# Attention stage: ScalarE takes the exponentials of a chunk's rows right behind that chunk's hi copy, and no longer behind the hi copy of the next chunk

## The chip, the cores and the metric

One core of a Trainium2 chip. The metric is the device time of one execution of the whole program, in microseconds; three runs of the kernel before gave 2290.93, 2291.99 and 2295.94 us, median 2291.99. The numbers of the profile come from one more execution, taken with the hardware profiler.

## What is computed

One transformer layer in fp32: adaptive norm and projections, a causal "forgetting" attention, a short convolution, an output projection, and a mixture of experts (32 experts, 4 for each token). Only the attention matters here. It has 8 heads of 64 columns over 1024 positions:

```
s = einsum('bhqd,bhkd->bhqk', q_block, k[:q1]) * scale      # a block is 128 queries
s = s + cum[q] - cum[k];  s = where(k_pos <= q_pos, s, -inf)
p = softmax(s);  out = p @ v[:q1]
```

The layer starts with `rms_norm(x) * (1 + sc1) + sh1`, where `sc1`, `sh1` and four more vectors come from `silu(c) @ w_ada`; part of that product is made on GpSimd beside the attention.

## The kernel before, in words

The program runs in four stages, each an `nc.Block()` with one instruction stream per engine and a meeting of all engines at its end: projections, attention (`attention_block`, L682), mixer, experts. Every engine takes its instructions strictly in the order written; semaphores tie the streams together.

**Rows and chunks.** Head h has 8 query blocks i = 0 to 7; row block n = 8h + i needs scores of width 128(i+1). Four blocks form a unit (i = 0 to 3, and i = 4 to 7). The probabilities of a unit are transposed key block by key block; one such step is a chunk. A head has 12 chunks, k = 0 to 11: k = 0 to 3 are the first unit (transposed width 512, 384, 256, 128) and k = 4 to 11 the second (512 five times, then 384, 256, 128). There are 96 chunks; below, c is the number over all heads and k the number within a head.

**What a chunk does**, engine by engine:
- TensorE: `turn(c)` transposes (L943), into one of three PSUM banks used in a ring; at k = 3 and 7 `fold_out` of the unit before (L970); then `scores(n)` for the row blocks in `scored[c]` (L928 to L931), into one of two pairs of banks, which waits for `exp(n-2)`; then `values(c-2)` (L959), the product with v of two chunks ago.
- ScalarE: `pthi`, the hi copy of the transposed chunk (L850), which waits for `turn(c)`; at k = 1 and 5 `copy_out` of the unit before (L841); then exponentials (L833), each with a read of the row sum behind it; and at 8 of the chunks from c = 48 on (every fifth: 48, 53, 58, 63, 68, 73, 78, 83) a copy of a piece of `w_out` for the next stage (L859).
- VectorE: `ptlo`, the lo part (L893), which waits for the hi copy of this chunk; at k = 3 and 7 `finish` of the unit before (L880, L883); then `lowest(n)` for the rows in `scored[c]` (a row reduction of the scores, L873), on which `exp(n)` waits; at k = 3 also a reciprocal for the mixer (L869), which stands behind the rest.

**Which rows in which chunk.** `scored` (L707 to L711) puts one row block into each of eight chunks: i = 6 and 7 of this head at k = 0 and 1, and of the next head i = 0, 1, 2, 3 at k = 4 to 7, i = 4 at k = 9, i = 5 at k = 11. Chunks 2, 3, 8 and 10 have none. The first six row blocks come ahead of chunk 0. `turn` of chunk k = 4 waits until i = 7 has its exponential, and that of k = 0 until i = 3 of its head has it.

**ScalarE's order before.** In chunk c it makes the hi copy of c and only then the exponentials of the rows scored in chunk c-1 (L854):

```
for n in scored[c - 1] if c else ():
    exp(n)
```

GpSimd meanwhile works through 16 pieces of `w_ada` (L818, L820, two buffers); SyncE loads q, k and v of later heads (L784 to L796), each when the scores or values of an earlier head are done.

Of the kernel before, what the change touches and what calls it, by code (L numbers as in the profile page):

```python
# [681 lines left out]
def attention_block(nc, s, a):  # L682
# [10 lines left out]
    NCH = len(chunks)  # L693
# [4 lines left out]
    def first(c):  # L698
        u, kt = chunks[c]
        return max(0, kt - QB * (u % 2))  # L700

    def through(u):
        return sum(QB * (v % 2 + 1) for v in range(u + 1))
# [3 lines left out]
    scored = {c: [] for c in range(NCH)}  # L707
# [11 lines left out]
    def copied(c):  # L719

        u, kt = chunks[c]
        return u - 1 if kt == 1 and u else None
# [16 lines left out]
    with ExitStack() as ctx:  # L739
# [23 lines left out]
        def probs(n):  # L763
            h, i = n // NT, n % NT
            return pr_short[:, i, :] if i < QB else pr_long[h % 2][:, i - QB, :]

        def scores_bank(n):
            L = (n % NT + 1) * P
            return psum[:, 2 * (n % 2):2 * (n % 2) + 2, :].rearrange("p b n -> p (b n)")[:, 0:L]

        with nc.Block() as block:
            @block.sync
            def _(sp):
                def load_values(h):

                    sp.dma_start(vhl[h % 2][:, :, :].bitcast(F32),
                                 s.v_d[:, h, :, :].rearrange("(t p) s n -> p t (s n)", p=P)).then_inc(v_in[h % 2], 16)

                load_values(0)
                for h in range(1, H):  # L780
                    i, rows = h % 2, slice(h * HD, (h + 1) * HD)
                    if h >= 2:
                        sp.wait_ge(s_mm, NT * (h - 1))
                    sp.dma_start(q1[i][0:HD, :].bitcast(F32), s.q_d[0, rows, :]).then_inc(qk_in[i], 16)  # L784
                    sp.dma_start(q1[i][HD:P, :].bitcast(F32), s.q_d[1, rows, :]).then_inc(qk_in[i], 16)
                    for half in (0, HD):
                        sp.dma_start(k1[i][half:half + HD, :].bitcast(F32), s.k_d[0, rows, :]).then_inc(qk_in[i], 16)
                    if h == 1:
                        sp.wait_ge(pad_ok, 2)
                    sp.dma_start(q2[i][0:HD, :].bitcast(F32), s.q_d[0, rows, :]).then_inc(qk_in[i], 16)  # L790
                    sp.dma_start(k2[i][0:HD, :].bitcast(F32), s.k_d[1, rows, :]).then_inc(qk_in[i], 16)
                    for dst, src in ((q2, s.extq_d), (k2, s.extk_d)):
                        sp.dma_start(dst[i][HD:HD + 4, :].bitcast(F32), src[h, :, :]).then_inc(ext_in[i], 16)
                    if h >= 2:
                        sp.wait_ge(pv_mm, through(2 * h - 3))
                    load_values(h)  # L796
                    if h == 2:
                        sp.dma_start(s.slab[:, :, :], a["w_out"][0].rearrange("(k p) n -> p k n", p=P)[:, :, 0:s.HALF]
                                     ).then_inc(slab_in, 16)
                sp.wait_ge(slab_in, 16)  # L800
# [23 lines left out]
            @block.scalar  # L824
            def _(act):
                def exp(n):
                    h, i = n // NT, n % NT
                    act.wait_ge(mn_ok, n + 1)
                    if i < QB and h >= 1:
                        act.wait_ge(pt_mm, through(2 * h - 2))  # L830
                    if i >= QB and h >= 2:
                        act.wait_ge(pt_mm, through(2 * h - 3))
                    nc.scalar.activation(probs(n)[:, 0:(i + 1) * P], scores_bank(n), ACT.Exp, bias=mn[:, n:n + 1],  # L833
                                         scale=-1.0, accum_out=rsum[:, n:n + 1]).then_inc(exp_ok, 1)

                def copy_out(u):

                    act.wait_ge(pv_mm, through(u))
                    if u >= 2:
                        act.wait_ge(fold_mm, u - 1)  # L840
                    nc.scalar.activation(outT[u % 2][:, :], psum[:, OB, :], ACT.Copy).then_inc(outT_ok, 1)  # L841

                for n in early:
                    exp(n)
                for c in range(NCH):
                    w = (QB - first(c)) * P
                    act.wait_ge(pt_mm, c + 1)
                    if c >= R:
                        act.wait_ge(pv_mm, c - R + 1)
                    nc.scalar.activation(pthi[c % R][:, 0:w], psum[:, TB + at_ring["chunk", c] % 3, 0:w],  # L850
                                         ACT.Copy).then_inc(pthi_ok, 1)
                    if copied(c) is not None:
                        copy_out(copied(c))
                    for n in scored[c - 1] if c else ():  # L854
                        exp(n)
                    if c in split_at:
                        k = split_at.index(c)
                        act.wait_ge(slab_in, 16)
                        nc.scalar.activation(s.whi0[:, k, :], s.slab[:, k, :], ACT.Copy)  # L859
                for n in scored[NCH - 1]:  # L860
                    exp(n)
                copy_out(NU - 1)

            @block.vector
# [1477 lines left out]
```

## Time and profile before

| | us |
|---|---|
| median of three runs | 2291.99 |
| profiled execution, its time | 2300.91 |
| profiled execution, its span | 2299.2 |
| TensorE busy | 2178.1 (95%) |
| VectorE busy | 1756.1 (76%) |
| ScalarE busy | 1358.2 (59%) |
| GpSimd busy | 815.7 (35%) |
| attention stage | 380.2 to 547.7 |

Busy time is the sum of the durations of an engine's instructions. TensorE's mean granted clock over the execution was 0.975 of full speed. The attention stage is 167.5 us of the span, 7%; most of the rest is the expert stage.

### The profile page before, as it was taken

Reading aid. Unit: us, or ns where it says so; the run is one execution under the profiler, and the core shown is the slowest. Engines: PE = TensorE matmul, PEld = TensorE weight load, DVE = VectorE, ACT = ScalarE, POOL = GpSimd, SP = SyncE. Lnnn points to the kernel's source line nnn. Section 1 sums busy time; section 2 is a strip of 40 time slices with the busy share of each in tenths; the row PEclk is TensorE's granted clock in tenths of the full one; section 3 lists DMA queues with packets and bytes.
Section 4 is the critical chain, followed back from the end, with each engine's and each line's share of the span. In section 5 each row is a group of like instructions: output and inputs, shape, how many; then the busy total and the mean of one; then the engine's idle time right before and its main releaser. Section 6 shows DMA issues by size and latency. Waiting matters only on the chain.

```text
span 2299.2 us, 37071 instructions
## 1 busy us (share of the span) xinstructions
PE 2178.1 (95%) x10302; PEld 1799.2 (78%) x10303; DVE 1756.1 (76%) x2165; ACT 1358.2 (59%) x1859; POOL 815.7 (35%) x804
## 2 busy tenths in 40 slices
PE   5999997888977899999999999999999999999997
PEld 4678885776865788888888888888888888888885
DVE  5683422676775799977799977788999779798897
ACT  4332211575325577766667766676777666677675
POOL 2263003885134234432224422142444322144241
PEclk9899998899988999999999999999999999999999
DMA  7233205883336899997789988797999878899794
GB/s 268 87 115 138 60 19 121 239 230 109 115 125 235 285 367 365 379 355 271 267 295 374 384 295 269 237 358 270 387 376 371 324 265 310 286 359 386 258 382 159
DMA packets 299090, 603.19 MB, mean 262 GB/s; under 512 B 24720, under 2 KB 46240, under 8 KB 295392
## 3 DMA queue, kind: packets, MB, share of 16 engines
q1 hardware_dynamic: 270912, 528.95, 64.1%
q0 software_dynamic: 27072, 69.40, 10.9%
q10 hardware_dynamic: 1056, 4.19, 0.5%
q8 instruction: 28, 0.46, 0.1%
q14 instruction: 22, 0.18, 0.0%
HBM read 563.71 MB, written 44.53 MB: 265 GB/s over the span
## 4 chain that ended last, share of the span: by engine, by line
PE 65%; DMA 2%; issue 1%; DVE 0%; POOL 0%; POOLq 0%; DVEq 0%; ACT 0%; ACTq 0%
PE psum L2255 60%; PE psum L2194 2%; PE psum L2237 2%; PE psum L2202 2%; DMA d_xg<-xn_d,d_entry 1%; DMA d_entry<-list_d 1%; POOL d_spare L1846 0%; POOL d_roww L1903 0%; DVE d_wlo L2073 0%; DVE d_yst L2126 0%; DVEq L1738 0%; ACT d_whi L1930 0%; POOLq L1689 0%; POOLq L1690 0%; POOLq L1842 0%
## 5 line engine op out<-in xcount | busy, mean ns | idle before, releaser
L2073 DVE TENSOR_TENSOR d_wlo<-d_raw,d_whi 128x1024 fp32r<-128x1024 f32 x578 | 676.7, 1219 | 127.7 <-ACT d_whi L1930 125.4
L1930 ACT ACTIVATE d_whi<-d_raw 128x1024 fp32r<-128x1024 f32 x578 | 579.8, 1054 | 62.7 <-PE psum L2255 49.7
L2255 PE MATMUL psum<-d_whi,d_xthi 128*128 128x512 f32 x1152 | 455.5, 395 | 6.1 <-issue 6.1
L2255 PE MATMUL psum<-d_whi,d_xtlo 128*128 128x512 f32 x1152 | 450.2, 391 | 0.0
L2255 PE MATMUL psum<-d_wlo,d_xthi 128*128 128x512 f32 x1152 | 449.9, 391 | 0.0
L1835 POOL DMA_INDIRECT out_dram<-d_yst,d_dest x49 | 149.7, 3055 | 665.2 <-DVE d_yst L2126 660.5
L2073 DVE TENSOR_TENSOR d_wlo<-slab,d_whi 128x1024 fp32r<-128x1024 f32 x292 | 343.8, 1219 | 21.6 <-ACT d_whi L1930 19.2
L1930 ACT ACTIVATE d_whi<-slab 128x1024 fp32r<-128x1024 f32 x292 | 292.3, 1054 | 7.7 <-PE psum L2255 6.1
L2255 PEld LDWEIGHTS psum<-d_whi,d_xthi 128*128 128x128 f32 x1152 | 217.3, 189 | 51.8 <-issue 8.0
L2255 PEld LDWEIGHTS psum<-d_whi,d_xtlo 128*128 128x128 f32 x1152 | 217.1, 188 | 46.3
L2255 PEld LDWEIGHTS psum<-d_wlo,d_xthi 128*128 128x128 f32 x1152 | 217.4, 189 | 43.6
L2255 PE MATMUL psum<-d_whi,d_athi 128*128 128x512 f32 x576 | 228.7, 397 | 0.0
L2255 PE MATMUL psum<-d_whi,d_atlo 128*128 128x512 f32 x576 | 224.6, 390 | 0.0
L2255 PE MATMUL psum<-d_wlo,d_athi 128*128 128x512 f32 x576 | 224.5, 390 | 0.0
L1972 ACT ACTIVATE d_athi<-psum 128x512 fp32r<-128x512 f32 x72 | 43.1, 599 | 181.6 <-PE psum L2202 170.9
L2255 PE MATMUL psum<-d_whi,d_xt 128*128 128x512 f32 x384 | 150.3, 391 | 0.0
L2255 PE MATMUL psum<-d_wlo,d_xt 128*128 128x512 f32 x384 | 150.1, 391 | 0.0
L2255 PEld LDWEIGHTS psum<-d_whi,d_atlo 128*128 128x128 f32 x576 | 108.2, 188 | 23.1
L1819 POOL DMA_INDIRECT d_xg<-xn_d,d_entry x48 | 68.2, 1422 | 162.0 <-DMA d_entry<-list_d 152.3
L2255 PEld LDWEIGHTS psum<-d_wlo,d_athi 128*128 128x128 f32 x576 | 108.3, 188 | 21.0
L2255 PEld LDWEIGHTS psum<-d_whi,d_athi 128*128 128x128 f32 x576 | 108.3, 188 | 20.0
L1826 POOL DMA_INDIRECT d_rowt<-topw_d,d_entry x72 | 95.6, 1328 | 41.7 <-POOL d_dest L1857 28.2
(351 smaller groups left out, 4010.8 us busy)
## 6 DMA issues: line engine op xcount, KB each, us to landing
slab<-in_w_gate_up_dram SPq DMA_DIRECT2D x144, 1024.0 KB, 8.4
d_raw<-in_w_gate_up_dram SPq DMA_DIRECT2D x144, 1024.0 KB
d_raw<-in_w_down_dram SPq DMA_DIRECT2D x144, 1024.0 KB
b_wp<-in_w_ada_dram POOLq DMA_DIRECT2D x16, 1024.0 KB, 9.4
slab<-in_w_in_dram SPq DMA_DIRECT2D x12, 1024.0 KB, 5.4
d_bias_rows<-in_b_gate_up_dram SPq DMA_DIRECT2D x12, 1024.0 KB
d_bias_rows<-in_b_down_dram SPq DMA_DIRECT2D x12, 512.0 KB
a_xin<-in_x_dram ACTq DMA_DIRECT2D x2, 2048.0 KB
```

What stands on the lines that cost most here:

```text
L1819: pool.indirect_dma_start(out=xg[b][:, :], out_offset=None, in_=src[:, :], in_offset=bass.IndirectOffsetOnAxis(ap=index, axis=0)).then_inc ...
L1826: pool.indirect_dma_start(out=rowt[b][:, :], out_offset=None, in_=s.topw_d[:, :], in_offset=bass.IndirectOffsetOnAxis(ap=entry[b][0:ROWS[b ...
L1835: pool.indirect_dma_start(out=s.out, out_offset=bass.IndirectOffsetOnAxis(ap=dest[b][:, :], axis=0), in_=yst[b][:, :], in_offset=None, com ...
L1930: nc.scalar.activation(whi[n % NW][:, part, :], raw[n % NRAW][:, part, :], ACT.Copy).then_inc(whi_ok, 1)
L1972: nc.scalar.activation(athi[:, 4 * i:4 * i + 4, :].rearrange("p k n -> p (k n)"), psum[:, 6, :], ACT.Copy).then_inc(athi_ok, sh)
L2073: nc.vector.tensor_tensor(wlo[n % NW][:, part, :], raw[n % NRAW][:, part, :], whi[n % NW][:, part, :].bitcast(F32), ALU.subtract).then_inc ...
L2194: mm = nc.tensor.transpose(turned_x[:, k, :], xg[b][:, k * P:(k + 1) * P], s.ident[:, :])
L2202: mm = nc.tensor.transpose(psum[:, 6 + b, t * P:(t + 1) * P], act_t[b][:, t * P:(t + 1) * P], s.ident[:, :])
L2237: mm = nc.tensor.matmul(to[0:ROWS[b], :], pick[:, 0:ROWS[b]], bhl[:, at:at + SL], start=False, stop=last)
L2255: mm = nc.tensor.matmul(to, m_[:, KH * h + k, :], w_[n % NW][:, k, :], start=(h == 0 and k == 0 and q == 0 and not loaded), stop=(h == 1 a ...
```

## The change

In chunk c ScalarE now makes the hi copy of c, then `copy_out` where there is one, and then the exponentials of the rows scored in the same chunk. The loop behind the last chunk goes, because nothing is left for it. The other engines' streams, the buffers and the number of instructions stay as they are.

```diff
                     if copied(c) is not None:
                         copy_out(copied(c))
-                    for n in scored[c - 1] if c else ():
+                    for n in scored[c]:
                         exp(n)
                     if c in split_at:
                         k = split_at.index(c)
                         act.wait_ge(slab_in, 16)
                         nc.scalar.activation(s.whi0[:, k, :], s.slab[:, k, :], ACT.Copy)
-                for n in scored[NCH - 1]:
-                    exp(n)
                 copy_out(NU - 1)
```

## Rows read from the trace of the kernel before

**Rows 1.** Busy time by stretch: stretch, length, each engine's busy us, TensorE clock, DMA.

```profile
380.20:547.70 167.50, 142.74 (x864) 121.18 (x864) 108.93 (x200) 104.95 (x249) 141.99 (x50) 0.92 0.75 206
```

**Rows 2.** Waits in 380 to 550: who waited for whom, us, times, longest.

```profile
PE psum L943 <- ACT b_pr_long L833: 4.7, 8, 1.8
PE psum L928 <- ACT b_pr_short L833: 3.7, 9, 0.6
PE psum L928 <- ACT b_pr_long L833: 3.6, 7, 0.9
```

**Rows 3.** Timeline, end of the stage: start, length, engine, line, operation.

```profile
541.52 4.58 POOL L820 TENSOR_TENSOR modacc<-modacc,b_wp 128x2048 f32<-128x2048 f32 x1
547.21 0.43 DVE L883 TENSOR_TENSOR attn<-psum,b_rsum 128x256 f32<-128x256 f32 x1
```

**Rows 4.** Timeline 501 to 520: instructions of one head on ScalarE and VectorE.

```profile
501.59 0.36 ACT L833 ACTIVATE b_pr_short<-psum,b_mn 128x128 f32<-128x128 f32 x1
501.93 0.60 ACT L850 ACTIVATE b_pthi<-psum 128x512 fp32r<-128x512 f32 x1
...
503.76 0.60 ACT L850 ACTIVATE b_pthi<-psum 128x512 fp32r<-128x512 f32 x1 [0.78 <-PE psum L943]
...
504.39 0.69 DVE L893 TENSOR_TENSOR b_ptlo<-psum,b_pthi 128x512 fp32r<-128x512 f32 x1 [0.67 <-ACT b_pthi L850]
...
505.00 0.17 DVE L880 RECIPROCAL b_rsum<-b_rsum 128x4 f32<-128x4 f32 x1
...
505.54 0.68 DVE L873 TENSOR_REDUCE b_mn<-psum 128x1 f32<-128x512 f32 x1
...
510.73 0.29 DVE L893 TENSOR_TENSOR b_ptlo<-psum,b_pthi 128x128 fp32r<-128x128 f32 x1 [0.79 <-ACT b_pthi L850]
...
510.94 0.95 DVE L873 TENSOR_REDUCE b_mn<-psum 128x1 f32<-128x768 f32 x1
...
511.92 0.90 ACT L833 ACTIVATE b_pr_long<-psum,b_mn 128x768 f32<-128x768 f32 x1 [0.73 <-DVE b_mn L873]
...
515.96 0.63 ACT L859 ACTIVATE whi<-slab 128x512 fp32r<-128x512 f32 x1
516.48 0.38 ACT L850 ACTIVATE b_pthi<-psum 128x256 fp32r<-128x256 f32 x1
...
516.74 1.12 ACT L833 ACTIVATE b_pr_long<-psum,b_mn 128x1024 f32<-128x1024 f32 x1
516.89 0.42 DVE L893 TENSOR_TENSOR b_ptlo<-psum,b_pthi 128x256 fp32r<-128x256 f32 x1 [1.41 <-ACT b_pthi L850]
...
517.83 0.29 ACT L850 ACTIVATE b_pthi<-psum 128x128 fp32r<-128x128 f32 x1
...
518.16 0.29 DVE L893 TENSOR_TENSOR b_ptlo<-psum,b_pthi 128x128 fp32r<-128x128 f32 x1 [0.84 <-ACT b_pthi L850]
...
518.91 0.94 DVE L869 RECIPROCAL crs<-crs 128x128 f32<-128x128 f32 x1
...
519.77 0.63 DVE L893 TENSOR_TENSOR b_ptlo<-psum,b_pthi 128x512 fp32r<-128x512 f32 x1
```

**Rows 5.** Timeline: hi copies of chunks 7, 14 and 86.

```profile
407.64 0.60 ACT L850 ACTIVATE b_pthi<-psum 128x512 fp32r<-128x512 f32 x1 [1.89 <-PE psum L943]
...
419.32 0.38 ACT L850 ACTIVATE b_pthi<-psum 128x256 fp32r<-128x256 f32 x1
...
534.65 0.38 ACT L850 ACTIVATE b_pthi<-psum 128x256 fp32r<-128x256 f32 x1
```

**Rows 6.** A wait of TensorE for a load (timeline).

```profile
441.74 0.48 PE L928 MATMUL psum<-b_k,b_q 128*128 128x128 f32 x1 [2.00 <-DMA b_k<-k_d]
```

**Rows 7.** Busy time by stretch, with TensorE's clock.

```profile
440.00:445.00 5.00, 3.26 (x15) 3.26 (x16) 2.00 (x4) 0.96 (x2) 3.54 (x1) 0.65 1.08 250
445.00:450.00 5.00, 4.84 (x25) 4.06 (x25) 2.57 (x6) 3.08 (x9) 4.62 (x3) 0.67 1.02 274
...
499.28:518.48 19.20, 16.62 (x111) 14.04 (x110) 13.45 (x26) 13.42 (x33) 16.40 (x6) 1.00 0.78 213
```

## The prediction, made before the changed kernel ran

> **What bounds the stage now.** I read the busy times by stretch first, then the waits, then the timeline of one head. The edit touches ScalarE's order between 380 and 547.7 us and nothing else, so only that stage counts. There TensorE is busy 142.7 of 167.5 us, VectorE 108.9, ScalarE 105.0, GpSimd 142.0 [rows 1]: no engine is full, TensorE is nearest. The waits show what it lacks: it waits for an exponential 3.7 + 3.6 + 4.7 = 12.0 us in all [rows 2], because scores(n) needs exp(n-2), and turn of chunk k = 4 needs the exponential of i = 7. A head takes 19.2 us: between the hi copies of chunks 14 and 86, six heads apart, lie 534.65 - 419.32 = 115.3 us [rows 5]. The stage ends with VectorE's last write at 547.64; GpSimd, which does its own work beside it, ends at 541.52 + 4.58 = 546.10 [rows 3], 1.5 us earlier, and the next stage waits for both.
>
> **What the order of before buys.** In chunk c ScalarE copies hi(c), then waits for nothing of this chunk: the exponential it takes is of the chunk before. Meanwhile VectorE makes lo(c) and the reduction of the new rows. The two engines work side by side, one chunk apart.
>
> **What the edit makes of it.** exp(n) now stands ahead of hi(c+1), and it needs the reduction of n, which stands on VectorE behind lo(c), which needs hi(c). So in each of the eight scored chunks of a head everything is in one file: hi(c), lo(c), reduction, exp(n), and only then hi(c+1). ScalarE sits still during lo and reduction, VectorE during the exponential and the next hi copy. Behind the waiting exponential are queued the hi copies, copy_out and the copies of L859; for them wait VectorE's lo parts and then TensorE's values and the ring of banks. Nothing else moves: no DMA is on ScalarE's queue here, SyncE's loads hang on scores and values and so come at the heads' own pace, and no instruction is added.
>
> **The links, from the timeline of one head [rows 4].**
> - hi copy of 512 to lo: 504.39 - 503.76 = 0.63; of 256: 516.89 - 516.48 = 0.41; of 384, between them: 0.52 (estimate).
> - lo of 512 to what follows on VectorE: 505.00 - 504.39 = 0.61; lo of 128: 510.94 - 510.73 = 0.21; so 0.34 for 256 and 0.47 for 384 (estimates on that line).
> - finish ahead of a reduction: 505.54 - 505.00 = 0.54. lo of chunk 3 to lo of chunk 4, over finish and the reciprocal of L869: 519.77 - 518.16 = 1.61.
> - reduction: 0.68 at 512 and 0.95 at 768, so 0.135 for each 128 columns: 0.28 at 128, 1.22 at 1024. Over i = 0 to 7: 8 x 0.75 = 6.0.
> - reduction to exponential: 511.92 - (510.94 + 0.95) = 0.03.
> - exponential with its read, to the next instruction on ScalarE: 501.93 - 501.59 = 0.34 at 128, 517.83 - 516.74 = 1.09 at 1024. Over i = 0 to 7: 8 x 0.715 = 5.7.
>
> **One head in the new order**, from hi copy to reduction in each scored chunk:
> - k = 4 (i = 0), counted from hi of chunk 2: lo(2) after 0.41, lo(3) 0.34 later, lo(4) 1.61 later, reduction 0.61 later: 2.97. (turn of chunk 4 starts on the exponential of i = 7; its hi copy is ready before VectorE comes to lo(4).)
> - k = 5 and 6: 0.63 + 0.61 = 1.24 each.
> - k = 7: 1.24 + 0.54 = 1.78.
> - k = 9 (from hi of chunk 8): 0.63 + 0.61 + 0.47 = 1.71; hi of chunk 9 is made meanwhile.
> - k = 11 (from hi of chunk 10): 0.41 + 0.34 + 0.21 = 0.96.
> - k = 0: 1.24; k = 1: 0.52 + 0.47 = 0.99.
> Together 12.1. With the reductions 6.0, the exponentials 5.7 and 8 x 0.03 = 0.2 a head is 24.1 us, against 19.2: 4.9 more. copy_out (k = 1 and 5) falls into ScalarE's wait and costs nothing. TensorE has 16.6 us of work in a head [rows 7] and 24.1 us for it, and its inputs (exp(n-2), lo of three chunks back) come earlier than it needs them, so I take it as never late; what it costs if it is, is below as the clock. Its 12 us of waits for exponentials go or turn into waits that cost nothing; that gain is inside the chain, since I compare whole heads. So is the 2.0 us wait for a load at 441.7 [rows 6]: a load has over a head's time, and a head gets longer.
>
> **The sum over the stage.**
> - Up to hi of chunk 7 (407.64 before) nothing changes: TensorE waits for the first loads and then works slowly, and the exponentials fit in. From there k = 7, 9, 11, 0, 1 run as above, to hi of chunk 14: before-reduction parts 1.78 + 1.71 + 0.96 + 1.24 + 0.99 = 6.68; reductions of i = 3 to 7 0.68 + 0.82 + 0.95 + 1.09 + 1.22 = 4.76; exponentials 0.66 + 0.77 + 0.88 + 0.98 + 1.09 = 4.38; links 0.15; 16.0 in all, so 423.6, against 419.3: +4.3.
> - Six heads: 6 x 24.1 = 144.6 against 115.3: +29.3.
> - The copies of L859: 516.48 - 515.96 = 0.52 each. Five of the eight stand right behind an exponential, on the chain: 2.6. At c = 58 and 68 part is covered by VectorE (0.34 and 0.28 left), at c = 63 all of it: +3.2. (The 115.3 has them already.)
> - The tail from hi of chunk 86: before, 547.64 - 534.65 = 12.99. Now the exponential of i = 7 is already done when hi(86) starts, 1.09 + 0.26 earlier than before; lo(88) gains less, as VectorE has lo, finish and the reciprocal ahead of it: about -1.1.
> Sum: 4.3 + 29.3 + 3.2 - 1.1 = +35.7 us. GpSimd's end at 546 no longer matters. The profiled span goes from 2299.2 to about 2334.9 and its time from 2300.9 to 2336.6. The median of the runs is 8.9 us under the profiled time; I carry the difference over: 2292.0 + 35.7 = **2327.7 us**, slower by 1.6%. Bounds: every link is read off one place or put on a line between two, so about 1 us a head either way, 7 in all. The lower end has one thing more: some of what I put in file may lie beside something after all; a quarter of the loss hidden would be 9 us less.
>
> **Rival 1, faster or no change: the earlier exponentials feed TensorE.** The waits speak for it: 12.0 us of TensorE's idle time end with an exponential [rows 2]. It is what happens if reduction n is ready when hi(c+1) could start, that is, if hi(c) to end of reduction (1.5 us at i = 0, 2.5 at i = 7) is no longer than TensorE's time from turn(c) to turn(c+1). It would return up to 12 us, but GpSimd's chain ends at 546.10 and lets the stage end only 1.5 us sooner: 2290.5, within 0.2%. Against it: the price of a chunk is not when its exponential starts but that hi(c+1) stands behind it, 0.3 to 1.1 us more. The Trainium skill ("Perfetto Trace Analysis", Optimization Strategies) says to speed up whatever blocks an idle matmul engine; read that way the edit is right, and it would give this rival's time. The blocking instruction does not get faster here, it only changes places with one that two other engines wait for.
>
> **Rival 2: the same chain, and TensorE's clock falls.** At 441.7, after a wait of 2.0 us [rows 6], the granted clock fell; it was 0.65 and 0.67 in the means of the two stretches of 5 us there, so at the lower of its two levels (1.2 GHz) for some 7 us of the ten [rows 7]. In the new order TensorE is busy 16.6 of 24.1 us, 69%, against 87% in rows 7, with single waits up to about 1.6 us (ahead of turn of chunk 4). In 7 us it has 4.8 us of work at full clock and 9.7 at half, so a fall costs at most 2.7 us; one fall in each of six heads costs up to 16, more likely half of it, as part is covered: +8, 2336. The Trainium skill ("TensorE: Matmul & The Clock Gate", What's actually happening) has the low clock as the default that activity lifts; the trace agrees in so far as the clock is 1.00 throughout rows 7's head of 87% and falls at the load wait, but has no stretch of this stage at 69%.
>
> **Rival 3: the edit shows up only in part** (several links overlap, or the old order had stalls that the new one saves and that I don't see): half to two thirds of the sum, +18 to +24, 2312.
>
> **Chances.** The forecast 0.67, rival 2 0.18, rival 3 0.10, rival 1 0.05. Less than 0.2% (4.6 us) either way can't be told from no change. Faster by more than that: 0.02 (GpSimd's end stands against it); no change 0.04; slower 0.94. The range for eight in ten is 2317 to 2343: links 7 us either way, the clock's cost at the top, part of rival 3 at the bottom.
>
> **What would show it.** In the changed profile: the hi copies of chunks 14 and 86 about 145 + 3 us apart; hi copies waiting for nothing while ScalarE's idle time stands in front of exponentials and ends with the reduction (before, it stood in front of hi copies and ended with TensorE); VectorE's idle time in front of lo parts; TensorE waiting for lo parts or for ScalarE in every chunk; GpSimd ending near 546 and then idle for some 37 us; the later stages as long as before. A head of about 19 us would refute the chain; a head of 24 with clock 1.00 refutes rival 2; a loss sitting in the expert stage would make the whole account wrong.

## The result and the profile after

The changed kernel takes 2340.52 us (median of four runs, 2338.55 to 2341.22) against 2293.38 for the kernel before in the same comparison: ratio 1.0196, 95% interval 1.018 to 1.0212. That is a loss of 45 us by the ratio (41 to 49) and of 47 us by the two medians. The forecast was 2327.7 us, a loss of 35.7, with a range of 2317 to 2343: the direction, the place and the mechanism hold; the loss came out 9 to 11 us larger than forecast, and the time 12.8 us above it.

The changed kernel's page, span and busy time of each engine:

```profile
span 2336.9 us, 37071 instructions
PE 2188.3 (94%) x10302; PEld 1807.1 (77%) x10303; DVE 1757.3 (75%) x2165; ACT 1358.5 (58%) x1859; POOL 814.8 (35%) x804
```

ScalarE and VectorE have hardly more work than before (1358.5 against 1358.2 us, 1757.3 against 1756.1). TensorE makes as many matmuls as before and is busy 10.2 us longer with them (2188.3 against 2178.1): its mean granted clock is 0.86 from 380 to 584, against 0.92 in [rows 1]. The rest of the time is in the waits. First those of the kernel before, in 380 to 550 (who waited for whom, us, times, longest):

```profile
DVE b_ptlo L893 <- ACT b_pthi L850: 42.9, 57, 1.7
ACT b_pthi L850 <- PE psum L943: 40.2, 44, 6.6
ACT b_pr_long L833 <- DVE b_mn L873: 8.7, 18, 1.4
ACT b_pr_short L833 <- DVE b_mn L873: 1.8, 3, 0.9
```

Then those of the changed kernel's attention stage:

```profile
DVE b_ptlo L891 <- ACT b_pthi L850: 87.6, 72, 2.1
POOL c_dump L1133 <- POOLq L771: 46.9, 1, 46.9
ACT b_pr_long L833 <- DVE b_mn L871: 46.3, 31, 1.8
ACT b_pr_short L833 <- DVE b_mn L871: 35.0, 28, 3.1
ACT b_pthi L850 <- PE psum L941: 16.0, 15, 1.8
PE psum L957 <- issue: 15.7, 6, 3.0
PE psum L926 <- ACT b_pr_long L833: 8.0, 8, 1.4
```

ScalarE now stands 46.3 + 35.0 = 81.3 us in front of exponentials until the reduction is there, where it stood 8.7 + 1.8 = 10.5 us before; its idle time in front of hi copies falls from 40.2 to 16.0. VectorE stands 87.6 us in front of lo parts until the hi copy is there, against 42.9: each waits while the other works. GpSimd waits 46.9 us for the stage to end.

One scored chunk (k = 6) in the changed kernel's timeline, the answer to [rows 4]:

```profile
499.99 0.59 ACT L850 ACTIVATE b_pthi<-psum 128x512 fp32r<-128x512 f32 x1
...
500.61 0.69 DVE L891 TENSOR_TENSOR b_ptlo<-psum,b_pthi 128x512 fp32r<-128x512 f32 x1 [1.64 <-ACT b_pthi L850]
...
501.21 0.55 DVE L871 TENSOR_REDUCE b_mn<-psum 128x1 f32<-128x384 f32 x1
...
501.80 0.58 ACT L833 ACTIVATE b_pr_short<-psum,b_mn 128x384 f32<-128x384 f32 x1 [1.22 <-DVE b_mn L871]
...
502.37 0.59 ACT L850 ACTIVATE b_pthi<-psum 128x512 fp32r<-128x512 f32 x1
```

Hi copy, lo part, reduction, exponential, next hi copy: each begins when the one before is done. From one hi copy to the next it is 2.38 us; the links of the forecast (0.63 + 0.61 + 0.55 + 0.03 + 0.55) give 2.37.

The hi copies of chunks 14 and 86 and the last write, against [rows 5] and [rows 3] (here hi copies of two chunks are merged in a row, x2):

```profile
418.69 0.54 ACT L850 ACTIVATE b_pthi<-psum 128x256 fp32r<-128x256 f32 x2
...
569.84 0.54 ACT L850 ACTIVATE b_pthi<-psum 128x256 fp32r<-128x256 f32 x2
...
583.08 0.42 DVE L881 TENSOR_TENSOR attn<-psum,b_rsum 128x256 f32<-128x256 f32 x1
```

Six heads take 151.2 us instead of 115.3. The stage, counted from TensorE's first scores to VectorE's last write, is 583.50 - 377.02 = 206.5 us against 547.64 - 380.33 = 167.3: 39 us, where the medians say 47. Behind the stage both programs take as long: 1753.4 us to the end of the span in the changed kernel, 1751.6 in the one before. The gap between 39 and 47 was the first thing to settle.

### The profile page after: what moved, and what is told of

It reads as the page before. It is cut to its first block, busy times and chain, and to the rows that moved or that the text cites. A ratio compares the mean times of both kernels' runs of the same rounds, so it can differ in the third digit from the quotient of the medians.

```text
span 2336.9 us, 37071 instructions
## 1 busy us (share of the span) xinstructions
PE 2188.3 (94%) x10302; PEld 1807.1 (77%) x10303; DVE 1757.3 (75%) x2165; ACT 1358.5 (58%) x1859; POOL 814.8 (35%) x804
## 4 chain that ended last, share of the span: by engine, by line
PE 65%; DMA 1%; issue 1%; DVE 0%; POOL 0%; DVEq 0%; POOLq 0%; ACT 0%; ACTq 0%
PE psum L2253 61%; PE psum L2192 2%; PE psum L2235 2%; PE psum L2200 2%; DMA d_xg<-xn_d,d_entry 1%; DMA d_entry<-list_d 0%; DVE d_wlo L2071 0%; POOL d_spare L1844 0%; POOL d_roww L1901 0%; DVEq L1736 0%; ACT d_whi L1928 0%; DVE d_yst L2124 0%; DVE d_raw L2176 0%; DVE d_bhl L2169 0%; DVE d_y_two L2061 0%
## 5 line engine op out<-in xcount | busy, mean ns | idle before, releaser
L2253 PEld LDWEIGHTS psum<-d_whi,d_xtlo 128*128 128x128 f32 x1152 | 217.1, 188 | 46.3
L891 DVE TENSOR_TENSOR b_ptlo<-psum,b_pthi 128x512 fp32r<-128x512 f32 (+1 forms) x96 | 51.6, 555 | 87.7 <-ACT b_pthi L850 87.6
```

The source lines that it names most:

```text
L891: nc.vector.tensor_tensor(ptlo[c % R][:, 0:w], psum[:, TB + at_ring["chunk", c] % 3, 0:w], pthi[c % R][:, 0:w].bitcast(F32), ALU.subtract) ...
L2253: mm = nc.tensor.matmul(to, m_[:, KH * h + k, :], w_[n % NW][:, k, :], start=(h == 0 and k == 0 and q == 0 and not loaded), stop=(h == 1 a ...
```

## The experiments

Stage length below is always this: first scores to the last write of `attn`, or to GpSimd's last addition where that ends later. The edits are shown against the changed kernel unless the text says otherwise. "Six heads" is hi copy of chunk 14 to that of chunk 86, which leaves out the first load and the tail. Before: 115.3 and, profiled again, 112.1; changed: 151.2 and 150.6.

**Both kernels, profiled once more.** No edit.

> The kernel before, unchanged, profiled once more. The changed kernel lost 47 us by the medians but 39 us by the lengths of the attention stage in the two traces (167.3 and 206.5). Theory A: the profiled execution of before was one with slow loads in this stage (GpSimd's chain, the same 16 pieces, took 165.8 us there and 158 to 160 in five other traces), so in another execution the stage is about 160 us and the difference in stage length 46. Theory B: the stage is 167 us again, and the 8 us are lost outside it (start of the next stages).

> The changed kernel, unchanged, profiled once more. Theory A: the stage is 206 to 207 us again, since its file of copies, lo parts, reductions and exponentials leaves no load on the path but the first; heads of 24.8 us with the clock falling once a head. Theory B: it varies by several us too.

Measured: before 2296.71 us (ten runs; ratio to the other runs of it 1.0004, interval 0.9988 to 1.002), changed 2340.31 (one run). Timeline of the second trace of before: hi copies of chunks 14 and 86, GpSimd's last addition, the last write of `attn`.

```profile
418.09 0.38 ACT L850 ACTIVATE b_pthi<-psum 128x256 fp32r<-128x256 f32 x1
...
530.23 0.38 ACT L850 ACTIVATE b_pthi<-psum 128x256 fp32r<-128x256 f32 x1
...
536.67 4.57 POOL L820 TENSOR_TENSOR modacc<-modacc,b_wp 128x2048 f32<-128x2048 f32 x1
542.79 0.43 DVE L883 TENSOR_TENSOR attn<-psum,b_rsum 128x256 f32<-128x256 f32 x1
```

With first scores at 381.26 the stage is 162.0 us, not 167.3. What differs is the loads. GpSimd's waits for its pieces of w_ada in the first and in the second trace of before:

```profile
POOL b_wp L818 <- DMA b_wp<-in_w_ada_dram: 17.6, 7, 7.3
```

```profile
POOL b_wp L818 <- DMA b_wp<-in_w_ada_dram: 11.6, 6, 6.4
```

In the second trace TensorE waits 1.26 us for the load at 440 instead of 2.00 [rows 6], and the clock (third figure from the end) stays at 1.00 behind it:

```profile
439.80 0.30 PE L928 MATMUL psum<-b_k,b_q 128*128 128x128 f32 x1 [1.26 <-DMA b_k<-k_d]
```

```profile
440.00:445.00 5.00, 4.42 (x36) 4.05 (x36) 2.78 (x7) 3.15 (x9) 4.61 (x3) 1.00 1.05 232
```

The head with this load takes 19.7 us there and 22.9 in the first trace; the other five take 92.5 and 92.4 us together. The changed kernel's stage is 206.0 us in its second trace, so the difference is 44.0 us there. Theory A holds for both: the trace on which the forecast was made was one with slow loads, and the changed kernel waits for no load of q and k but the first, that of head 1. Theory A's numbers were a stage of 160 us and a difference of 46; it is 162.0 and 44.0.

**Half of the edit each.** Only the short rows (i < 4), and only the long rows, behind their own chunk's hi copy:

```diff
# short rows                                   # long rows: < and >= exchanged
-                    for n in scored[c]:
-                        exp(n)
+                    for n in scored[c - 1] if c else ():
+                        if n % NT >= QB:
+                            exp(n)
+                    for n in scored[c]:
+                        if n % NT < QB:
+                            exp(n)
```

> Only the short rows (i = 0 to 3, scored in chunks k = 4 to 7) are taken behind their own chunk's hi copy; the long rows stay one chunk later as before. Theory A (hi copy, lo part, reduction and exponential stand in one file in every scored chunk, and each such chunk pays for it): from hi(4) to hi(8) a head goes from 6.6 us to about 9.9, some of it back behind hi(8) because the exponential of i = 3 is already done; net +2.8 a head for six heads and less for the first: about +17 us, 2310. Theory B (only the long exponentials are worth anything, the short ones fit into TensorE's pace): within 3 us of the kernel before. Theory C (the loss comes from TensorE's lower clock, which the late copy_out at k = 1 sets off): also close to the kernel before, because copy_out at k = 1 is where it was.

> Only the long rows (i = 4 to 7, scored in chunks k = 9, 11, 0, 1) are taken behind their own chunk's hi copy. Theory A: the rest of the changed kernel's loss, about 39 - 17 = 22 us of stage, so about 2314; if the two parts add up, the stage lengths of this run and of the one with the short rows exceed that of the kernel before by 39 us together. Theory B: nearly the whole loss, over 35 us. Theory C (clock): over 30 us, and the clock falls once a head. If the two parts overlap (slack of one covers the other) the sum of the two losses is clearly under 39.

Measured: short rows 2314.04 us against 2294.44 (ratio 1.0077, 1.005 to 1.0103), long rows 2328.32 (1.014, 1.0115 to 1.0165). Hi copies of chunks 14 and 86 with the short rows, then with the long rows:

```profile
420.16 0.39 ACT L850 ACTIVATE b_pthi<-psum 128x256 fp32r<-128x256 f32 x1
...
548.80 0.38 ACT L850 ACTIVATE b_pthi<-psum 128x256 fp32r<-128x256 f32 x1
```

```profile
421.12 0.54 ACT L850 ACTIVATE b_pthi<-psum 128x256 fp32r<-128x256 f32 x2
...
562.72 0.54 ACT L850 ACTIVATE b_pthi<-psum 128x256 fp32r<-128x256 f32 x2
```

Six heads: 128.6 and 141.6 us, 16.5 and 29.5 above the 112.1 of before; the stages are 181.3 and 196.3 us, 19.3 and 34.3 above 162.0. Both halves cost, so theory B falls for the short rows. Theory C does too: with the short rows the granted clock is 1.00 in all stretches of 5 us from 420 to 560, and the loss is there. By theory A the stage was to lose 17 and 22 us. The short half nearly fits; the long half costs 12 more, and with it the clock falls once a head, as theory C had it for these rows (over 30 us), so this pair does not part the two there; the next runs do. Over six heads the two add up to 46.0 where the whole edit costs 38.4, so each half alone also loses something that the whole edit does not. The excess of 7.6 us is +6.5 between hi(2) and hi(5), +4.7 between hi(10) and hi(12) and -5.1 between hi(8) and hi(10), with the rest spread; what makes it is not shown.

**The lo part out of the file.** The changed kernel, with VectorE's order turned:

```diff
+                    for n in scored[c]:
+                        lowest(n)
                     dve.wait_ge(pthi_ok, c + 1)
                     nc.vector.tensor_tensor(ptlo[c % R][:, 0:w], ...
                     if finished(c) is not None:
                         finish(finished(c))
-                    for n in scored[c]:
-                        lowest(n)
```

> The changed kernel, but VectorE takes the reduction of the new rows ahead of the lo part (and ahead of finish) of the same chunk. ScalarE's order is that of the changed kernel. Theory A: with the lo part out of the file, the exponential needs only TensorE's scores and the reduction, and the next hi copy no longer stands behind hi + lo + reduction + exponential: a head returns to 19 to 20 us, the stage to 167 to 175 us, the program to 2293 to 2300. Rival (the exponential ahead of the next hi copy is itself what costs, by 0.3 to 1.1 us in each scored chunk, whatever VectorE does): 8 x 0.7 = 5.7 us a head less at most what TensorE hides, so the stage stays at 195 us or more and the program over 2320.

The same turn in the kernel before:

> The kernel before, with ScalarE's order unchanged, but VectorE takes the reduction of the new rows ahead of the lo part and of finish. With the changed order of ScalarE this gave six heads in 106.0 us (17.7 each) and a stage set by GpSimd. Theory A (the order on VectorE is what matters; ScalarE's order is then of little weight): six heads in 104 to 109 us, the stage 159 to 161 us, set by GpSimd, program within 3 us of before. Rival (with the reduction first, the exponential behind its own hi copy is the better place, since it is ready by then): six heads in 111 us or more, as the exponential still waits for the next hi copy.

Measured: 2293.73 us against 2294.44 (ratio 0.9999, 0.9987 to 1.0011) in the changed order of ScalarE, 2295.62 against 2296.08 (0.9994, 0.9976 to 1.0011) in the old one. Timeline with both turned: hi copies of chunks 14 and 86, GpSimd's last addition, the last write, GpSimd's first instruction of the next stage.

```profile
417.28 0.54 ACT L850 ACTIVATE b_pthi<-psum 128x256 fp32r<-128x256 f32 x2
...
523.30 0.54 ACT L850 ACTIVATE b_pthi<-psum 128x256 fp32r<-128x256 f32 x2
...
534.80 4.49 POOL L820 TENSOR_TENSOR modacc<-modacc,b_wp 128x2048 f32<-128x2048 f32 x1
...
535.15 0.42 DVE L881 TENSOR_TENSOR attn<-psum,b_rsum 128x256 f32<-128x256 f32 x1
...
541.66 0.32 POOL L1133 MEMSET c_dump<- 128x256 f32 x1 [2.36 <-POOLq L771]
```

Six heads take 106.0 us, 6 less than before (17.7 a head; theory A said 19 to 20), and the whole loss is gone, though ScalarE's order is still the changed one. So the exponential ahead of the next hi copy costs nothing by itself here; it costs because its reduction stood behind the lo part of the same chunk, and so behind the hi copy. The rival fails by far. The attention is done at 535.57, GpSimd at 539.29: the stage is now set by GpSimd, 159.4 us. In the old order of ScalarE six heads are 108.7 us (theory A said 104 to 109) and the stage, again set by GpSimd, is 158.8. So with the reduction first the edit is worth 0.4 us a head in the other direction, by one trace each; the last pair of runs takes it up again.

**The late copy_out and the clock.** In the changed kernel copy_out at k = 1 stands behind hi(1), which stands behind the exponential of i = 6. Timeline: end of TensorE's work, ScalarE's copies, and TensorE's next product with v, which by the program waits for copy_out (the profile has "issue" there), then two stretches with the clock:

```profile
513.50 0.41 PE L941 MATMUL psum<-ident,b_pr_short 128*128 128x128 f32 x2
...
515.37 0.48 ACT L850 ACTIVATE b_pthi<-psum 128x384 fp32r<-128x384 f32 x1
515.74 0.60 ACT L841 ACTIVATE b_outT<-psum 128x512 f32<-128x512 f32 x1
...
516.43 0.77 PE L957 MATMUL psum<-b_pthi,b_vhl 128*128 128x512 f32 x1 [2.53 <-issue]
```

```profile
515.00:520.00 5.00, 3.57 (x14) 3.21 (x15) 2.54 (x6) 3.50 (x9) 4.68 (x3) 0.57 1.01 268
520.00:525.00 5.00, 5.00 (x31) 4.74 (x30) 3.05 (x6) 2.37 (x6) 4.92 (x2) 0.75 1.05 234
```

TensorE waits 2.53 us, the clock goes to the lower level (1.2 GHz) 0.7 us before the wait ends and is back at 522.5, and turn of chunk 4, on which hi(4) waits, runs in between. From head to head the wait is 2.5 to 3.1 us long and the fall comes between 2.5 us before and 1.3 us behind its end. Two edits went at this. The first takes copy_out at k = 0:

```diff
-                    if copied(c) is not None:
+                    if copied(c) is not None and c % per_head != 1:
                         copy_out(copied(c))
+                    if c and c % per_head == 0:
+                        copy_out(copied(c + 1))
```

> The changed kernel, but the copy_out that stood at k = 1 (behind hi(1), and so behind the exponential of i = 6) is taken at k = 0, between hi(0) and that exponential. In the changed kernel TensorE waits 2.5 us for it ahead of values of chunk 0, and the clock falls once a head there; from hi(2) to hi(5) a head then takes 4.3 us instead of 3.7. Theory A (the fall is set off by this one wait): the clock stays at 1.00 in most heads, about 0.6 us a head and about 1 us of the tail come back: stage 206.5 to about 202, program 4 us below the changed kernel. Rival (TensorE's low share of busy time is enough): the clock still falls once a head and the stage stays within 1 us of 206.5. Rival 2: the wait for the values of chunk 11 moves into ScalarE's file ahead of the exponential of i = 6 and costs up to 1 us a head.

Measured: 2335.34 us, ratio 1.0177 (1.0152 to 1.0202); stage 586.37 - 380.58 = 205.8 us, where theory A said 202 and the rival within 1 us of 206.5. The clock falls once a head all the same, only later. Stretches of that kernel:

```profile
470.00:475.00 5.00, 3.41 (x19) 3.09 (x19) 3.19 (x7) 2.24 (x5) 4.92 (x2) 0.68 1.01 324
475.00:480.00 5.00, 5.00 (x29) 4.81 (x28) 2.51 (x6) 2.92 (x8) 4.68 (x3) 0.64 1.04 229
```

The one wait of 2.5 us is gone, but others have come ahead of fold_out and turn of chunk 4 (1.29 and 1.59 us in the head shown, with the fall in the second; 1.81 and 1.39 in the next, with the fall between them). So a wait of 2.5 us is not needed for the fall, and this run does not price the clock. By the medians the program is 5.2 us below the changed kernel, about the 4 that theory A said, but the traces put that behind the stage: 1747.0 us from its end to the end of the span, against 1753.4 and 1751.6. The median therefore does not speak for theory A; why the rest is shorter is open. The second edit fills TensorE's idle time and moves nothing else. The scores of i = 7 are made three times (the work is added, the result is the same):

```diff
-                    for c0 in range(0, L, 512):
+                    again = 2 if i == NT - 1 else 0
+                    for c0 in [0, 512] * again + list(range(0, L, 512)):
```

> The changed kernel, but TensorE makes the scores of i = 7 (chunk k = 1) three times over, with the same result, in the time in which it otherwise waits 2.5 us for copy_out; the reduction of i = 7 starts 2.9 us behind the first copy's end, and the two more copies take 1.7 us, so nothing is late by it. Theory A (the lower clock behind that wait is what makes hi(2) to hi(5) 4.3 us instead of 3.7): the clock stays at 1.00 in most heads, hi(2) to hi(5) is 3.6 to 3.8 us in them, six heads take 147.5 us instead of 150.6 to 151.2, and the stage 202 us instead of 206. Rival (the clock has no part in it, the hi copies of chunk 4 are late for another reason): clock 1.00, but hi(2) to hi(5) still 4.3. If the clock falls all the same the run does not tell.

Measured: 2326.79 us against 2296.29, ratio 1.0123 (1.0108 to 1.0139). Timeline (hi copies of chunks 14 and 86, last write), and a stretch with the clock:

```profile
423.90 0.54 ACT L850 ACTIVATE b_pthi<-psum 128x256 fp32r<-128x256 f32 x2
...
571.60 0.54 ACT L850 ACTIVATE b_pthi<-psum 128x256 fp32r<-128x256 f32 x2
...
583.45 0.43 DVE L881 TENSOR_TENSOR attn<-psum,b_rsum 128x256 f32<-128x256 f32 x1
```

```profile
495.00:500.00 5.00, 3.90 (x34) 3.54 (x32) 3.25 (x8) 2.38 (x6) 4.60 (x4) 1.00 1.08 276
```

The clock is 1.00 in every stretch from 410 to 560. Six heads take 147.7 us (expected 147.5), the stage 202.8. In each of the six heads hi(2) to hi(5) is 3.56 us, where the changed kernel has 3.8 to 4.3; every other stretch of a head is as long as there. So the clock costs 3 to 3.5 us over six heads: rival 2 of the forecast is real, beside the chain and not in its place. By the medians this kernel is 13.7 us below the changed one, 10 more than its stage gives. Its trace shows 7 to 9 us less behind the stage, in the experts (1578.7 us from the first product there to the end, against 1583 to 1589 in eleven other traces). TensorE spends 19 us of the experts at the lower clock in it and 23 to 29 in the others, which at half speed explains 5 us at most; what made both differ is open.

**A version that beats both.** The reduction first, ScalarE in the changed order, and the last of GpSimd's 16 pieces on VectorE, as one fused instruction ahead of the last finish; and the same with ScalarE's old order:

```diff
-                for r in range(NPIECE):
+                for r in range(NPIECE - 1):
...
+                dve.wait_ge(wp_in[last % 2], 16 * (last // 2 + 1))
+                dve.wait_ge(pool_own, 2 * last)
+                nc.vector.scalar_tensor_tensor(s.modacc[:, cols], wp[last % 2][:, :], s.csilu[:, k:k + 1],
+                                               s.modacc[:, cols], ALU.mult, ALU.add)
                 finish(NU - 1)
```

> Both changes at once (exponentials behind their own hi copy, reduction ahead of the lo part), and the last of the 16 pieces of w_ada, which GpSimd ended 3.7 us after the attention, goes to VectorE as one fused instruction ahead of the last finish. Theory A (GpSimd's chain is what sets the stage's end there): the stage ends 2.5 to 3.7 us earlier than with GpSimd doing it, 156 us against 159.4, and the program is 3 us below that kernel and 3 to 5 below the kernel before. Rival: the fused instruction (2048 columns, some 2.2 us by the 1.2 us that 1024 columns take VectorE elsewhere) delays the last finish by as much, and the stage ends no earlier.

> The fastest kernel so far (reduction ahead of the lo part, last piece of w_ada on VectorE) with ScalarE's order of before, so that the edit alone is undone there. By the two traces with the reduction first, a head takes 17.7 us in the changed order and 18.1 in the old one: the attention ends 2 to 3 us later than the 157.4 us of the fastest, at about 159 to 160, and the program is 0 to 3 us slower than it, still faster than before or equal. Rival (in that setting ScalarE's order does not matter): attention 157 to 158 us, and the same time.

Measured: 2291.10 us against 2296.08, ratio 0.9976 (0.9959 to 0.9992), and with ScalarE's old order 2293.93 against 2296.29, 0.9989 (0.998 to 0.9999). The end of the stage in the first of the two:

```profile
528.60 4.59 POOL L820 TENSOR_TENSOR modacc<-modacc,b_wp 128x2048 f32<-128x2048 f32 x1
...
534.95 2.34 DVE L903 SCALAR_TENSOR_TENSOR modacc<-b_wp,csilu,modacc 128x2048 f32<-128x2048 f32 x1
537.42 0.18 DVE L878 RECIPROCAL b_rsum<-b_rsum 128x4 f32<-128x4 f32 x1
537.63 0.42 DVE L881 TENSOR_TENSOR attn<-psum,b_rsum 128x256 f32<-128x256 f32 x1
```

GpSimd ends at 533.19 and no longer sets the end; the fused instruction ends at 537.29, within VectorE's wait for the last fold. The stage is 538.05 - 380.67 = 157.4 us (156 expected; this trace has two load waits, 5.2 and 1.9 us). The program is 0.24% faster than before, barely clear of no change; without the last piece moved the interval was 0.9987 to 1.0011, which touches this one, so what the move alone is worth to the program is not shown. In the old order 159 to 160 us were expected and the stage is 163.5. Of the 6.1 us between the two, 4.0 lie ahead of the hi copy of chunk 14, 1.4 in the six heads (109.2 against 107.8) and 0.7 behind them. The 4.0 go with the clock: the wait for the first load is 5.2 us in the changed order and 6.4 in the old one, and the first scores of head 1 come 19.9 and 20.1 us into the stage, but behind it the clock is back at 404 in the changed order and not by 412 in the old one. The same stretch in the changed order, then in the old one (the granted clock is the third figure from the end):

```profile
408.00:412.00 4.00, 4.00 (x25) 3.17 (x24) 3.01 (x7) 2.88 (x8) 1.41 (x2) 1.00 0.94 273
```

```profile
408.00:412.00 4.00, 4.00 (x17) 3.51 (x17) 1.54 (x4) 0.91 (x3) 1.58 (x3) 0.50 0.88 286
```

The six heads repeat the pair above. Without the one head that waits for a load, the other five take 88.5 us in both traces of the changed order and 90.7 and 90.6 in both of the old one: with the reduction first, the edit shortens a head by 0.4 us. Whether that is worth anything to the program is not shown, as the intervals of the two ratios overlap.

## Why the prediction was right, and where it was short

- **The mechanism.** "Everything is in one file" is shown three ways: by the links (2.38 against 2.37 us in a chunk; from hi(8) to the next head's hi(2) 12.8 us by the sum and 12.8 in the heads without a copy of L859), by the waits, and by taking the lo part out of the file, which brings everything back.
- **A head.** 24.1 us and the copies of L859 were forecast, 147.8 for six heads. With the clock held up they take 147.7, with 24.08 us in each of the two heads without such a copy. That agreement is better than the bounds that I gave the links.
- **GpSimd as the cap.** Forecast for rival 1: whatever the attention saves, GpSimd's chain keeps. With the reduction first the attention ends 3.7 us before GpSimd, and the program time does not move.
- **Mis-sized, first term: the kernel before.** The sum took 115.3 us for six heads [rows 5] from one trace; the second gives 112.1. The first had slow loads, a 2.0 us wait at 441.7 [rows 6] and the lower clock behind it. I named both, and said that the gain from losing them is in the sum, but not that another execution of the kernel before may lose them as well. The 8.9 us between the profiled time and the median were the sign of it, and I carried them over as if profiling had cost them. This is the step that makes most of the miss: the forecast of the profiled time was 2336.6 us and 2338.55 was measured, 2.0 off, but the changed kernel's profiled run is its fastest, 2.0 us below its median and not 8.9 above it. 2.0 + 2.0 + 8.9 are the 12.8 us, up to rounding. The first 2.0 is in part luck: against the first trace the stage lost 39.2 us and not 35.7, the rest of the program 1.8, and the stage happened to begin 3.3 us earlier. Counting from the second trace, the same chain gives 144.6 + 3.2 - 112.1 = 35.7 for six heads instead of 32.5.
- **Mis-sized, second term: the clock.** I gave it 18% as a rival in place of the forecast. It comes on top: hi(2) to hi(5) is 4.2 to 4.3 us in four of the changed kernel's heads instead of 3.62, about 3 us in all. (The trace of before had single stretches of 5 us as little busy as a head of the new order, such as 390 to 395 with 3.08 us of work at a clock of 0.97, but none that lasts.) The step that failed is "copy_out (k = 1 and 5) falls into ScalarE's wait and costs nothing". On ScalarE that is so; but values of the next unit waits for it, TensorE stands 2.5 us where I had 1.6 as its longest wait, and the clock falls there.
- **The tail and the first chunks.** Forecast -1.1 and +4.3. From hi(7) to hi(14) the changed kernel takes 16.0 us in both traces and the one before 11.7 in both, which is the +4.3. What lies ahead of hi(7) differs by -1.6 in the first traces and +1.3 in the second, with different first loads. The tail is 13.0 us before, 13.7 and 13.0 changed, and 12.3 with the clock held up: 0.7 of the 1.1 was there, and at the lower clock it is lost again. By the second traces 5.6 + 38.4 + 0.0 = 44.0 us of stage, within the 41 to 49 us of the ratio's interval.
- **Rival 1's argument.** It would hold if the reduction were ready early. With the reduction moved it was, and the changed order is then no loss. The reason that I gave against it, that hi(c+1) stands 0.3 to 1.1 us further back behind the exponential whatever else happens, is refuted by the same run: with that still so, a head took 17.7 us.

## What to carry to other kernels

An instruction moved ahead of another on an in-order engine must have its inputs ready at that place. Follow them back through the other engines: if they lead to what this engine has just done in the same step, two engines that worked side by side now take turns. If a move like this is wanted, move the producer of its input first (here the reduction ahead of the lo part). And take a second profiled execution, or the run nearest the median, before subtracting from it: one trace can carry several microseconds of slow loads that the changed kernel will not have.

## What the runs showed of the hardware beside this

- TensorE's granted clock fell at single waits of 2.0 us (kernel before) and 2.5 to 3.1 us (changed), and at two waits of 1.3 to 1.8 us close together (copy_out moved). It stayed up over single waits of 1.26 us (kernel before, second trace) and 1.89 us (last piece on VectorE). With that wait filled by repeated scores, it stayed at 1.00 from 410 to 560.
- Behind a first wait for a load of 5.2 and of 6.4 us it came back at 404 in one trace and not by 412 in the other; the stretch up to chunk 14 is 4.0 us longer there.
- The same 16 loads of w_ada cost GpSimd 17.6 and 11.6 us of waits in two traces of the kernel before, and 10.2 to 13.6 in the other kernels that leave all 16 to it.
